# A hybrid diffusion layer on one core: block products for the DeltaNet projections, gate columns moved ahead, modulation rows moved into the Hyena stage

## The reference, cut to what matters

```python
hx = rmsnorm(x, norm1_g) * (1.0 + sc1x) + sh1x          # hc likewise for the context
p = hx @ w_in                                           # hc only through the DeltaNet columns
qkv = silu(short_conv(p[..., :3 * 512], dn_conv_w, rows))
q, k, v = heads(qkv); q = l2norm(q) * 128 ** -0.5; k = l2norm(k)
z = p[..., 3 * 512:4 * 512]                             # later silu(z)
gcols = p[..., 2048:2064]                               # 16 columns: beta and decay, 2 directions x 4 heads
beta = sigmoid(gcols[:, :, 0]); g = -exp(a_log) * softplus(gcols[:, :, 1] + dt_bias)
mod_x = silu(c) @ ada_w + ada_b                         # six rows of 1024: sh1, sc1, g1, sh2, sc2, g2
```

## Time and profile before

| | us |
|---|---|
| median of 3 runs | 4094.59 (4093.77 to 4094.99) |
| the profiled execution | 4092.06 |
| its span, first to last instruction | 4090.1 |
| mean granted TensorE clock | 0.960 of full speed |
| DeltaNet projections | 107 to 664 |
| gate stage, with the start of the recurrence | 664 to 737 |
| Hyena and short convolution projections | 1335 to 1643 |

### The profile page before, as it was taken

How to read it: one execution, slowest core, us unless ns; L and a number is a source line. 1 busy time by engine, 2 the same in 40 slices (tenths; PEclk the granted TensorE clock), 3 DMA queues, 4 the chain that set the end, 5 groups by cost and what they waited for, 6 DMA issues and landing times. The chain is left out here.

```text
span 4090.1 us, 46175 instructions
## 1 busy us (share of the span) xinstructions
PE 3764.6 (92%) x17138; PEld 2374.5 (58%) x17138; DVE 1857.3 (45%) x2914; ACT 1030.4 (25%) x2185; POOL 779.2 (19%) x590
## 2 busy tenths in 40 slices
PE   6999997999999999887999999998967999999994
PEld 2444442888888444344444444434546888888883
DVE  4433332555555443645322222214345666666664
ACT  4444452444444111031111111111211111111112
POOL 1122120333443000031011111112231122211220
PEclk8999998999999999998999999999978999999997
DMA  7333221222221111695111111115433665566654
GB/s 264 121 104 109 75 79 36 95 80 77 82 82 47 57 52 41 187 245 165 58 53 59 54 52 52 52 48 182 155 145 114 200 219 190 192 221 196 206 175 175
DMA packets 296762, 490.36 MB, mean 120 GB/s; under 512 B 20534, under 2 KB 175833, under 8 KB 296145
## 3 DMA queue, kind: packets, MB, share of 16 engines
q1 hardware_dynamic: 276959, 425.86, 31.2%
q0 software_dynamic: 11808, 42.79, 4.1%
q10 hardware_dynamic: 7829, 19.46, 1.5%
HBM read 377.27 MB, written 110.77 MB: 119 GB/s over the span
## 5 line engine op out<-in xcount | busy, mean ns | idle before, releaser
L627 PE MATMUL bank<-hT,wq 128*128 128x512 f32 x1024 | 450.1, 593 | 0.0
L627 PEld LDWEIGHTS bank<-hT,wq 128*128 128x128 f32 x1024 | 192.5, 190 | 225.0 <-issue 224.3
L2067 PE MATMUL bank<-hT,raw_w 128*128 128x512 f32 x576 | 260.7, 595 | 9.4 <-DMA raw_w<-in_w_in 9.4
L2976 PE MATMUL bank<-xeT,raw_e 128*128 128x128 f32 x2304 | 267.8, 275 | 0.0
L2976 PEld LDWEIGHTS bank<-xeT,raw_e 128*128 128x128 f32 x2304 | 263.6, 192 | 7.2 <-issue 7.2
L2259 POOL TENSOR_TENSOR mg<-mg,sg_m 128x512 f32<-128x512 f32 x64 | 88.1, 1377 | 719.4 <-DVE sg_m L2161 719.4
L2067 PEld LDWEIGHTS bank<-hT,raw_w 128*128 128x128 f32 x576 | 110.0, 191 | 147.9 <-issue 138.3
L736 POOL TENSOR_SCALAR sg<-tmp 128x512 f32<-128x512 f32 (+1 forms) x76 | 107.6, 1417 | 455.6 <-DVE tmp L752 371.9
L2976 PE MATMUL bank<-T_e,U 128*128 128x128 f32 x1536 | 176.7, 275 | 0.0
L2976 PEld LDWEIGHTS bank<-T_e,U 128*128 128x128 f32 x1536 | 174.1, 192 | 0.0
L2067 PE MATMUL bank<-zT,S 128*128 128x512 f32 x384 | 172.6, 592 | 0.0
(11 more groups left out here) (458 smaller groups left out, 7042.4 us busy)
## 6 DMA issues: line engine op xcount, KB each, us to landing
raw_e<-in_exp_w_gate SPq DMA_DIRECT2D x16, 3072.0 KB
raw_e<-in_exp_w_up SPq DMA_DIRECT2D x16, 3072.0 KB
raw_e<-in_exp_w_down SPq DMA_DIRECT2D x16, 3072.0 KB
ada<-in_ada_w SPq DMA_DIRECT2D x12, 2048.0 KB, 10.1
raw_w<-in_w_in SPq DMA_DIRECT2D x24, 1024.0 KB, 5.4
fa_d<-az ACTq DMA_DIRECT2D x48, 264.0 KB
sp_in<-fa_d SPq DMA_DIRECT2D x66, 192.0 KB, 4.8
raw_h<-in_w_in SPq DMA_DIRECT2D x12, 1024.0 KB, 5.3
```

Of the source, the lines that this page charges most:

```text
L627: last = pe.matmul(PS[g % 4][:, 0:width(n)], wq[:, kind, k, :], h_of(k, toff(n), width(n)), start=(k == 0), stop=(k == KD - 1))
L2067: mm = pe.matmul(bank[:, :], lhs[:, k, :], rhs[:, k, :], start=first and k == 0, stop=k == 3, skip_group_check=not first)
L2976: mm = pe.matmul(bank[:, f * P:(f + 1) * P], lhs[:, k, f * P:(f + 1) * P], rhs[:, k, :], start=fresh and k == 0, stop=k == 3, skip_group_c ...
```

## The change

**DeltaNet projections.** The 76 units are ordered into 16 quads (half of the tokens, pair of heads, kind), each of 256 columns by 1024 tokens, made in seven block products. In the first half of the tokens, kinds 0 to 2 also carry two context units, which are made plainly (`context`), behind the quad. The weights come as 256 columns at a time into three buffers, asked for when quad Q has ended for quad Q + 3. The pieces of the slots stay as they were but for their sources (the sums in `cb`, the bank X, or the context copy `cx`), and are issued between the products by `behind`: the last two slots of the quad before, its context slots, and the first two of this one.

**Gate columns.** They are made first in this stage, with 128 tokens stationary and the 16 columns moving; the small chain runs on VectorE and ScalarE ahead of quad 0's slots, the six sums behind P5 of quad 1. The gate stage is gone.

**Modulation rows.** They move into the Hyena stage's first six quads: SP loads 64 tiles of 128x512 into a ring of six, which lies in parts of `x0T` and `zT` that are not yet used; ScalarE scales each in place, POOL adds them, TensorE sums over partitions between the products of quads 1 to 5, VectorE adds bias and gain on single rows, and SP stores the rows before the second half of the quads.

```diff
+        quads = [(tp, hp, kind) for tp in range(2) for hp in range(2) for kind in range(4)]
+        with_ctx = lambda Q: quads[Q][0] == 0 and quads[Q][2] < 3
+            units += [(2 * hp + r, kind, 2 * tp + 1 + c) for r, c in ((0, 0), (1, 1), (0, 1), (1, 0))]
+            if with_ctx(Q):
+                units += [(2 * hp, kind, 0), (2 * hp + 1, kind, 0)]
...
+            def in_turn(Q):
+                late = list(range(first[Q - 1] + 2, first[Q])) if Q else []
+                return late[0:1], late[1:2], late[2:]
...
 # SP
+                    for Q in range(NQ):
+                        while done < first[Q] - 4:
+                            store(done)
+                            done += 1
+                        if Q + RW < NQ:
+                            sp.wait_ge(c21_mm, Q + 1)
+                            if with_ctx(Q):
+                                sp.wait_ge(cx_mm, ctx_no[Q] + 1)
+                            load(Q + RW)
...
 # TensorE
+                    def gate_columns():
+                        pe.wait_ge(wg_in, 16)
+                        for c in range(STEPS):
+                            for k in range(KD):
+                                last = pe.matmul(PS[7][:, c * 16:(c + 1) * 16], h_of(k, c * P, P), wg[:, k, :], start=(k == 0), stop=(k == KD - 1))
+                        last.then_inc(gates_mm, 1)
...
+                    def behind(slots):
+                        for s in slots:
+                            if s - 2 in norm_no:
+                                norm_sum(s - 2)
+                            if s - 4 in turn_no:
+                                turn(s - 4)
+
+                    gate_columns()
+                    for Q in range(NQ):
+                        early, middle, rest = in_turn(Q)
+                        product(X(Q), w(Q, 0, 0), t(p, 0, 0), True).then_inc(p1_mm, 1)
+                        behind(early)
...
+                        if Q >= 1:
+                            pe.wait_ge(c12_ok, Q)
+                        product(Z, S1, T1, True).then_inc(p5_mm, 1)
+                        if Q == SUMS_AT:
+                            gate_sums()
...
+                        pe.wait_ge(p1s_ok, Q + 1)
+                        product(X(Q), S2, T2, False).then_inc(u2_mm, 1)
+                        behind(middle)
...
+                        product(Y, w(Q, 0, 1), t(p, 1, 0), True).then_inc(y_mm, 1)
+                        behind(rest)
...
+                        pe.wait_ge(u2s_ok, Q + 1)
+                        product(X(Q), S3, T3, False).then_inc(u3_mm, 1)
+                        behind([first[Q]])
...
+                        product(Z, S4, t(p, 1, 1), False).then_inc(z_mm, 1)
+                        pe.wait_ge(c22_ok, Q + 1)
+                        product(X(Q), w(Q, 1, 1), T4, False).then_inc(c21_mm, 1)
+                        behind([first[Q] + 1])
+                        if with_ctx(Q):
+                            context(Q)
...
 # ScalarE
+                    gate_values()
+                    for Q in range(NQ):
+                        early, middle, rest = in_turn(Q)
+                        kept(p1s, X(Q), p1_mm, c11_ok, p1s_ok, Q)
+                        behind(early)
+                        kept(p5s, Z, p5_mm, c22_ok, p5s_ok, Q)
+                        if Q == SUMS_AT:
+                            gate_exps()
+                        kept(u2s, X(Q), u2_mm, c12_ok, u2s_ok, Q)
+                        behind(middle)
+                        behind(rest)
+                        behind([first[Q], first[Q] + 1])
+                        if with_ctx(Q):
+                            context(Q)
...
 # VectorE
+                        behind(early)
+                        if Q + 1 < NQ:
+                            sum1(Q + 1)
...
+                            sum2(Q + 1)
+                        behind(middle)
+                        summed(Q, 0, Y, y_mm, p1s, p1s_ok, c11_ok)
+                        behind(rest)
+                        summed(Q, 1, X(Q), u3_mm, p5s, p5s_ok, c22_ok)
+                        if Q + 1 < NQ:
+                            sum3(Q + 1)
+                        behind([first[Q]])
+                        summed(Q, 2, Z, z_mm, u2s, u2s_ok, c12_ok)
...
 # the Hyena stage
+            NMOD, RM = 8, 6
+            tiles_before = [20, 34, 48, 62, 64, 64]
+            sums_behind = {(1, 5): (0, 1), (2, 2): (2,), (2, 6): (3,), (3, 2): (4,), (3, 6): (5,), (4, 2): (6,), (5, 2): (7,)}
+                    def load_tiles(q):
+                        for t in range(tiles_before[q - 1] if q else 0, tiles_before[q]):
+                            if t >= RM:
+                                sp.wait_ge(acc_ok, added(t - RM))
+                            b, k = divmod(t, KD)
+                            sp.dma_start(md[t % RM], A["ada_w"][0, k * P:(k + 1) * P, 2 * D + b * 512:2 * D + (b + 1) * 512]).then_inc(md_in[t % RM], 16)
...
+                        if q == QP:
+                            act.wait_ge(acc_ok, NMOD * (KD - 1))
+                            act.wait_ge(mod_st, 16 * NMOD)
+                        if q == 0:
+                            scale_tiles(tiles[0:RM])
+                            tiles = tiles[RM:]
                         kept(p1s, X(q), p1_mm, c11_ok, p1s_ok, q)
+                        scale_tiles(tiles[0:4])
                         kept(p5s, Z, p5_mm, c22_ok, p5s_ok, q)
                         kept(u2s, X(q), u2_mm, c12_ok, u2s_ok, q)
+                        scale_tiles(tiles[4:8])
                         middle(q, 0)
                         to_nat(q, 0)
+                        scale_tiles(tiles[8:])
                         to_nat(q, 1)
                         middle(q, 1)
...
+                            pool.tensor_tensor(acc[b % 3], md[(t - 1) % RM] if k == 1 else acc[b % 3], md[t % RM], ALU.add).then_inc(acc_ok, 1)
...
+                        if q == QP - 1:
+                            dve.wait_ge(mod_st, 16 * NMOD)
```

More of the change, by code:

```diff
@@ L520, in build @@
         conv_no = {g: c for c, g in enumerate(conv_units)}
-        NG = len(units)
         with ExitStack() as st:
-            TB, YB, SB, NTB = 3, 7, 4, 3
-            wq = sbt(st, "wq", [P, 4, KD, P])
+            TB, YB, SB, NTB, RW = 3, 7, 4, 3, 3
+            raw = sbt(st, "raw_d", [P, RW, KD, 2 * P])
+            S1, S2, S3, S4 = [sbt(st, n, [P, 4, P]) for n in ("S1_d", "S2_d", "S3_d", "S4_d")]
+            T1, T2, T3, T4 = [sbt(st, n, [P, 4, TW]) for n in ("T1_d", "T2_d", "T3_d", "T4_d")]
+            p1s, p5s, u2s = [sbt(st, n, [P, TW]) for n in ("p1s_d", "p5s_d", "u2s_d")]
+            cb, cx = sbt(st, "cb_d", [P, 3, TW]), sbt(st, "cx", [P, 2, CTX])
             tmp = sbt(st, "tmp", [P, TB, TW])
@@ L596, in _ @@
[L596 to L607, removed]
@@ L611, in _ @@
+                    while done < NG:
+                        store(done)
+                        done += 1
                     for b in range(YB):
@@ L617, in _, with product @@
                 def _(pe):
[L618 to L629, removed]
+                    def product(bank, lhs, rhs, first):
+                        for k in range(4):
+                            mm = pe.matmul(bank[:, :], lhs[:, k, :], rhs[:, k, :], start=first and k == 0, stop=k == 3, skip_group_check=not first)
+                        return mm
@@ L631, in norm_sum, with context @@
+                    def context(Q):
+                        pe.wait_ge(c11_ok, Q + 1)
+                        for r in range(2):
+                            for k in range(KD):
+                                last = pe.matmul(Y[:, r * CTX:(r + 1) * CTX], w(Q, r, k // 4)[:, k % 4, :], hTc[:, k, :], start=(k == 0), stop=(k == KD - 1))
+                        last.then_inc(cx_mm, 1)
                     def norm_sum(g):
@@ L667, in _ @@
+                    behind(range(first[NQ - 1] + 2, NG + 4))
                 @block.scalar
@@ L712, in to_nat, with behind @@
                         act.activation(nat[:, r % NTB, 0:w], PS[6 + r % 2][:, 0:w], ACT.Copy).then_inc(nat_ok, 1)
[L714 to L724 removed]
+                    def behind(slots):
+                        for s in slots:
+                            if s < NG:
+                                centre(s)
+                            if s - 5 in turn_no:
+                                to_nat(s - 5)
+                            if 1 <= s <= NG:
+                                logistic(s - 1)
+                            if s - 3 in norm_no:
+                                root(s - 3)
+                            if s - 1 in norm_no:
+                                square(s - 1)
+                    gate_values()
[4 more added lines that the diff above has]
+                        kept(p5s, Z, p5_mm, c22_ok, p5s_ok, Q)
+                        if Q == SUMS_AT:
+                            gate_exps()
[5 more added lines that the diff above has]
+                            context(Q)
+                    behind(range(first[NQ - 1] + 2, NG + 5))
```

(15 more changed lines are left out.)

421 lines of the change are left out of this document (256 added, 165 removed).

## The result

| | before | after |
|---|---|---|
| median, us | 4094.59 | 4068.35 (4063.3 to 4076.4, 5 runs) |
| ratio, 95% interval | | 0.9941 (0.9928 to 0.9954) |
| span of the profiled execution | 4090.1 | 4066.5 |

The change is worth 26 us. The forecast was 4044, a gain of 50.8; the time lies in the range given with it, between the forecast and rival 1 (4074).

A forecast was written before the change was run, and what follows sets the result against it. TensorE was taken to bound the DeltaNet and Hyena projections, with engines taking turns in the gate stage. DeltaNet's 610.8 - 545.0 = 65.8 us gain, less 15 for Hyena, gave 50.8 and 4044 us; range 4024 to 4087.

The forecast's parts named there:

- rival 1: DeltaNet gate columns run at the low clock throughout: 61.2 instead of 32.4 us, +30.5 in all, 4074 us; chance 0.28.
- Gate columns: DeltaNet stage, TensorE: 288 thin passes at 0.106 us are 30.6, plus 1.8 for a low-clock start: 32.4 us.
- the router's shape: Price source for the gate columns: the router's sixteen passes of the same shape took 1.70 us, 0.106 each.
- Products, context, norm sums, transposes: DeltaNet stage, TensorE: products 383.9 us, context 41.2, norm sums 30.8, transposes 15.4; waits inside the stage 24, rest 3.
- SP's queue, bank copies, weight sums: DeltaNet stage: stores late by up to a quad, ScalarE's copies and VectorE's sums not the bound; the queue costs nothing.
- rival 3: DeltaNet quads: every quad pays what context quads pay, 12 x 6.8 = 82 us, 4125 us; chance 0.06.
- Hyena stage: Modulation rows moved into the Hyena projections lengthen that stage by 15 us (bounds 7 and 35), of which sums 6.9.
- the start: Hyena stage's beginning: ScalarE scales six tiles before keeping p1s, which U2 wants; costs 2 us.
- the turn: Hyena stage, second half: VectorE and ScalarE wait until the eight rows are stored, p1s is wanted; costs 1 us.
- quad 3's transpose: Hyena stage: the fourth transpose of z wants a copy standing behind the last six tiles; costs 3 us.
- late copies: Hyena stage: the quads keep p5s and u2s behind late tiles; costs about 2 us (0 to 10).
- Rival 2: Hyena stage: the tiles pace it, coming 5 us late per quad and at the start, 20 more, 4064 us; chance 0.13.

The follow-up runs named there:

- the repeated columns: Changed kernel with gate columns reading their 16 weight columns eight times over, as a moving operand of 128, nothing more loaded: 4042.36 us, ratio 0.9872 to the kernel before.
- The warm start: Changed kernel with twelve unread passes of 512 columns ahead of the gate columns: 4071.68 us, ratio 0.9945 to the kernel before.
- the kernel with two long passes: Changed kernel with two unread passes of 512 columns behind each of the first 17 token tiles' gate columns: 4098.62 us, ratio 1.0009 to the kernel before.
- The split: Repeated columns with later slots behind U3, changed: half moved behind the product into Z, first slot too: 4017.91 us, ratio 0.9814 to the kernel before.

## Why the prediction was wrong, by its own steps
- **Gate columns, the step that failed.** "I take the router's shape, plus 1.8 for a start at the low clock: 32.4", with 61.2 as the other end; measured 60.4. What failed is the price of a pass, 0.106 us taken from a row at the full clock, against 0.21 at the granted 0.50 over nearly the whole run. The 1.8 for the start was about right: with the repeated columns the first 32 passes take 5.08 (110.06 to 115.14), where 32 x 0.112 are 3.6. Rival 1 is what happened: mechanism, place and price (+28.0 here, where it had 28.8, and 2.8 on the first product, where it had 1.7; together 30.8, and the rival said 30.5, so two small misses cancel). I had its evidence in hand, the sixty thin products at 0.50, and set it aside for idle time between them. The warm start shows that no idle time is needed, and the kernel with two long passes that thin passes in that measure win even against long ones. The router's row was the nearest in shape, but not in what surrounds it.
- **The case of thin passes.** The granted clock in the gate columns is 0.51 over 61 us in which TensorE is busy for 60.66. The Trainium skill (TensorE: Matmul & The Clock Gate, Why this matters for your kernels) names products with few rows as a case in which the clock falls back at every tile of the depth, and as a remedy either to run all tiles of the depth before the next DMA or to pad the rows. The case here is a neighbour of that one: the thin side is the moving operand, and no DMA stands between the tiles of the depth. The clock fell all the same, so the first remedy, which this loop already has, does nothing here; padding the moving side raised it (0.9872 against 0.9941).
- **Products, context, norm sums, transposes.** 472.6 by prices, plus 27 for waits, clock and rest: 499.6 against 500.9. Luck has a part in this. Inside, the idle waits were 14.8 (I had 20), the low clock took 6.2 (three stretches: 1.7 in quad 2, 2.8 in quad 5, 1.7 in quad 6), not 4, the slow first product 2.8, and some 4.5 remain where I had 3. The waits for squares stand in quads 1, 2, 5 and 6 alone, as forecast; but behind kind 2, where I had the transposes ready, one in quad 7 waited 1.5 us for ScalarE's copy `nat`. The product's 896 x 0.429 is 384.4, not 383.9, which changes nothing. The split shows that these waits and their clock together cost 24.1 us (654.70 to 630.62); as idle time they look like 14.8.
- **SP's queue, bank copies, weight sums**: cost nothing, as said. No wait of TensorE for them, and rival 3 did not occur.
- **Hyena stage.** +15 forecast, +8.6 measured. Against the kernel before, the sums are 6.9, the first product took 6.42 instead of 5.12 (+1.3) and the start waited 1.07 for u2s, where I had 2 for both; the turn waited 1.66 where I had 1. The 1.3 is not the tiles' doing: without any modulation the first product took 6.71. The 3 for quad 3's transpose and the 2 for late copies did not come. Taken off are 1.7, since the kernel before has two products of 5.37 here and the changed one has one, and 0.9 of a shorter wait for `fw` at the start of the stage behind (14.7 instead of 15.6); together 8.3 of the 8.6. Rival 2 fell: ScalarE waits 37.7 us for the tiles in `x0T` and 6.5 for those in `zT`, and of this only 0.8 reach TensorE, whose waits for ScalarE are 7.0 us, against 6.2 without tiles:
```profile
L1879 POOL TENSOR_TENSOR ycT<-ycT,x0T 128x512 f32<-128x512 f32 x32 | 47.0, 1469 | 17.1 <-ACT x0T L1661 12.5 <-POOL ycT L1879 0.5
L1661 ACT ACTIVATE x0T<-x0T,csil 128x512 f32<-128x512 f32 x44 | 30.1, 718 | 37.9 <-DMA x0T<-in_ada_w 37.7
...
L1788 DVE TENSOR_TENSOR S_h<-raw_h 128x512 f32<-128x512 f32 x12 | 11.3, 940 | 32.1 <-PE bank L1589 28.5 <-DMA raw_h<-in_w_in 3.0 <-DVE x0T L1771 0.3
```
GpSimd's add took 1.44 in the mean of all 56 (I took 1.4). VectorE's weight sum went from 0.69 to 0.94 in the mean, with single ones at 1.75, more than the 0.92 that I had; in the kernel without the adds it is 0.69 again. TensorE has no wait for a weight sum, as forecast.
- **The whole.** 50.8 forecast, less 30.8 for the clock in the gate columns, plus 6.4 in the Hyena stage, less 2.9 for the rest (4.1 behind the Hyena stage and 0.6 for the later start lost; 1.0 in the other terms of the DeltaNet stage and 0.8 in the recurrence gained): 23.5. The chance of 0.28 for rival 1 was too low beside 0.45 for the forecast.

## What to carry to other kernels
Price TensorE's work at the clock that its own neighbourhood gets: a row of the same shape is worth little if it stands between other passes. If many thin fp32 passes must run in a row, widen the moving operand; 128 columns instead of 16 cost almost nothing here at the full clock, reading the same columns several times loads nothing more, and it brought 60.4 us to 33.7. Count waits of 2 to 3 us on TensorE at more than their length (17.1 us for 10.7 in the one pair of kernels that shows it, some 1.6 times), and look for the instruction that is early in the queue before looking for a faster engine.

## What the runs showed of the hardware that I had not expected
- At full clock a pass with 128 stationary columns takes almost the same with 16 moving columns (0.106 beside whole products, 0.109 in the warm start) as with 128: in the kernel that reads its columns eight times, 256 passes from 115.14 to 143.73, 0.112 each, at a granted clock of 1.00 (the count of a window takes in the passes that its edges cut).
```profile
130.00:140.00 10.00, 10.00 (x92) 10.00 (x91) 0.00 (x0) 0.00 (x0) 0.00 (x0) 1.00 0.01 2
```
- TensorE's granted clock fell from 1.00 to 0.50 with not one idle microsecond, in the warm start; and with 34 long passes among 288 thin ones it stayed at 0.50 from 115 us on.
- 16 thin and 8 long passes at 1.00 take 5.22 us, 16 thin and 2 long at 0.50 take 5.12: four times the long work for 2% more time.
- In one execution, a wait of 2.15 us is followed by a product of 5.37 us and one of 2.12 by a product of 3.67; and of two waits of 2.87 us one costs 2.8 us of slow work behind it and the other none.
